# Two output norms of a 1-core transformer kernel, each cut into an early and a late part

## The chip, the core and the metric

One core of a Trainium2 chip runs the whole program as one launch. The metric is device time in microseconds, the median of several runs.

## What is computed

Two transformer blocks over 512 tokens of 1024 features, all float32. Each has an attention whose output is normed and goes through a projection:

```python
# block 1
o = concat([rms_norm(oa, g_out_a), rms_norm(ob, g_out_b)], axis=-1)   # two halves of 512 features
x = x + gate_m * (o @ w_out)                                          # then routing and 32 experts
# block 2
o = diff_attention(q, k_all, v_all, lam)                              # 8 heads of 128 features
o = rmsnorm(o, subln_g) * (1.0 - lam_init)                            # a norm for each head
y_attn = o.reshape(B, L, ATTN_OUT) @ w_branch_attn                    # then gates, w_out, PEER experts
```

`oa` comes from a sparse attention (top 128 keys chosen by an index score), `ob` from a forgetting attention.

## The kernel before

The program is a row of blocks, one for each stage, and each block ends with a barrier of all engines. Within a block every engine has its own instruction list, and semaphores order the lists. The token rows lie in `k.o` as 4 tiles (`TT`) of 128 tokens by 1024 features; the products want them feature by feature, as 8 chunks (`KC`) of 128 features by 512 tokens. A float32 product is done in three, from a high and a low part of either operand (`split_products`, lines 195 to 197).

Attention loops (`attention_stage`, `diff_attention_stage`). Each has n = 32 units of a pair of heads, or one head, by one token tile. The loop runs over t with the steps of one unit staggered: score at t, exponential at t (ScalarE, L927 or L2307), turn of the probabilities at t-2 (L777, L2212), copy of the turned ones (ScalarE, `copy_turned`, L935, L2315), weighing with the values at t-3 (L790, L2221), copy of the result to `k.o` at t-4 (VectorE, L825, L2262), its square and sum at t-5 (ScalarE, `square`, L956, L2327). In the first attention units 0 to 15 are `ob` (features 512 to 1023) and units 16 to 31 are `oa`; in the second the order is head by head, so units 28 to 31 are head 7.

Norm (`HeadNorm`, at the start of `out_projection_stage` and `mix_query_stage`, thus behind the barrier). VectorE sums the squares (L1000, L1002, L1003); ScalarE loads the root's table with an idle activation (L1033) and takes the root (L1035); VectorE inverts it (L1006). Then two engines scale the four token tiles in place: VectorE L1010, ScalarE L1040. TensorE turns all 32 pieces of 128 by 128 into the 8 banks of PSUM (L1025). ScalarE writes each chunk's high part (L1044), VectorE its low part (L1013).

Products. `first_products` does output chunks 0 and 1 together, kc by kc, so that it can follow the parts as they come. It writes banks 0 and 1, so it waits for the parts of chunks 0 and 1 before its first product. Later output chunks go through `chunk_products`. Weights stream through a ring of 4 tiles of 1 MB, each serving two output chunks. ScalarE splits off a tile's high part (`high_part`, L169), Pool its low part (`low_part`, L176), the latter raising `w_ready`, and SyncE loads the next tile (L145). In ScalarE's list the high part of the stage's second tile stands behind `norm.scalar`.

In the first out-projection SyncE also loads at the block's start: the routing weights, small tables, two experts (`w_expert_in` 2 x 2 MB, `w_expert_down` 2 x 1 MB, L1083, L1085), and then, once the rows are read (`norm.rows_read`), the table `before` (L1087) and the ring. VectorE at L1146 and TensorE at the bias product L1124 wait for all six of the small loads, `before` among them. Behind L1124 TensorE has the first routing logits (L1117), then output chunk 2, logits, chunk 3, and so on.

`keep_going` issues products of ones into an unused bank.

## Time and profile before

| quantity | value |
|---|---|
| median of 3 runs | 2797.2 us (2794.76 to 2803.7) |
| the profiled execution, its own time | 2801.7 us |
| its span in the trace | 2799.9 us |
| TensorE busy | 2669.2 us (95%) |
| VectorE busy | 1797.7 us (64%) |
| ScalarE busy | 1075.5 us (38%) |
| GpSimd (Pool) busy | 927.1 us (33%) |
| mean granted TensorE clock | 0.973 of 2.4 GHz |

Read it from the last column of a group of rows inward: a timeline row gives when a group of like instructions began, how long it took, and, in brackets, how long the engine sat idle ahead of it and what released it. TensorE is busy nearly always, so the place to look is where it is not. Matmul ends are modelled: a wide product shows 0.39 us but the next one starts 0.23 us after it. PEclk is the granted clock, 1.00 for 2.4 GHz and 0.50 for 1.2 GHz.

### The profile page before, as it was taken

What the parts mean: (1) busy time and instruction counts of PE and PEld (TensorE: products, weight loads), DVE (VectorE), ACT (ScalarE), POOL (GpSimd) and SP (SyncE); (2) the same over time, 40 slices, a digit from 0 to 9 for tenths busy, and PEclk for the clock granted to TensorE, in tenths of its full rate; (3) what the DMA queues carried; (4) which work ended last, traced back from release to release, by engine and by line L of the source; (5) the groups of instructions that cost most, each with busy time, mean ns of one, the idle gap of its engine ahead of it and who ended that gap; (6) DMA issues with size and microseconds to landing.
All of it is one profiled execution on the core that took longest, in us unless ns stands there. A gap on an engine that the chain in (4) does not pass through costs nothing. (4 is left out here: it accounts for less than half of the span.)

```text
span 2799.9 us, 37231 instructions
## 1 busy us (share of the span) xinstructions
PE 2669.2 (95%) x14205; PEld 2187.1 (78%) x14209; DVE 1797.7 (64%) x3171; ACT 1075.5 (38%) x1724; POOL 927.1 (33%) x468
## 2 busy tenths in 40 slices
PE   8997998889999999999899999999999999999998
PEld 5776775333477878878787899999999988888887
DVE  7958432111142538439744199997998967888987
ACT  3225734222243322147633233344555533333333
POOL 0011122222224330121142257886323233455542
PEclk9996999999999999999999999999999999999999
DMA  8830048999633345300322146886689799999995
GB/s 347 312 118 1 1 155 314 418 404 375 263 118 120 135 159 196 135 16 1 121 90 92 61 153 254 294 296 221 224 309 322 291 365 390 375 400 386 396 406 198
DMA packets 135470, 646.30 MB, mean 231 GB/s; under 512 B 21537, under 2 KB 22433, under 8 KB 91041
## 3 DMA queue, kind: packets, MB, share of 16 engines
q1 hardware_dynamic: 86224, 485.11, 46.0%
q0 software_dynamic: 48384, 158.38, 15.0%
q8 instruction: 85, 1.39, 0.2%
q10 hardware_dynamic: 720, 0.96, 0.1%
q14 instruction: 57, 0.46, 0.1%
HBM read 620.25 MB, written 75.50 MB: 248 GB/s over the span
## 5 line engine op out<-in xcount | busy, mean ns | idle before, releaser
L195 PE MATMUL psum<-h_hi,w_hi 128*128 128x384 f32 (+1 forms) x1808 | 665.9, 368 | 21.8 <-DVE h_lo L575 5.3
L197 PE MATMUL psum<-h_hi,w_lo 128*128 128x384 f32 (+1 forms) x1808 | 653.0, 361 | 0.0
L196 PE MATMUL psum<-h_lo,w_hi 128*128 128x384 f32 (+1 forms) x1808 | 652.2, 361 | 0.0
L176 POOL TENSOR_TENSOR w_lo<-ring,w_hi 128x2048 fp32r<-128x2048 f32 x45 | 211.2, 4693 | 729.7 <-ACT w_hi L169 546.4
L195 PEld LDWEIGHTS psum<-h_hi,w_hi 128*128 128x128 f32 x1808 | 342.8, 190 | 56.6 <-issue 27.0
L197 PEld LDWEIGHTS psum<-h_hi,w_lo 128*128 128x128 f32 x1808 | 342.2, 189 | 34.0
L196 PEld LDWEIGHTS psum<-h_lo,w_hi 128*128 128x128 f32 x1808 | 342.8, 190 | 32.7 <-issue 1.9
L2589 ACT ACTIVATE w_hi<-ring 128x2048 fp32r<-128x2048 f32 x127 | 242.5, 1909 | 214.6 <-PE psum L197 193.5
L195 PE MATMUL psum<-w_hi,a_hi 128*128 128x512 f32 x768 | 301.1, 392 | 3.9 <-DVE w_lo L2597 3.1
L197 PE MATMUL psum<-w_hi,a_lo 128*128 128x512 f32 x768 | 300.1, 391 | 0.0
L196 PE MATMUL psum<-w_lo,a_hi 128*128 128x512 f32 x768 | 300.1, 391 | 0.0
L2597 POOL TENSOR_TENSOR w_lo<-ring,w_hi 128x2048 fp32r<-128x2048 f32 x40 | 191.2, 4781 | 93.2 <-ACT w_hi L2589 91.7
L2628 POOL DMA_INDIRECT rows<-in_peer_u,row_index x88 | 131.1, 1489 | 261.7 <-DVE rows L2643 243.2
L2597 DVE TENSOR_TENSOR w_lo<-ring,w_hi 128x2048 fp32r<-128x2048 f32 x87 | 198.8, 2285 | 17.1 <-ACT w_hi L2589 17.1
L3227 ACT ACTIVATE a_hi<-hid_tiles 128x768 fp32r<-128x768 f32 x64 | 54.2, 847 | 348.4 <-PE psum L197 315.6
L1515 PE MATMUL psum<-w_expert_in,x_turn 128*64 128x512 f32 x768 | 171.5, 599 | 13.1 <-issue 10.9
L169 ACT ACTIVATE w_hi<-ring 128x2048 fp32r<-128x2048 f32 x64 | 122.3, 1912 | 135.7 <-PE psum L197 105.6
L195 PEld LDWEIGHTS psum<-w_hi,a_hi 128*128 128x128 f32 x768 | 145.0, 189 | 34.4 <-issue 4.6
L197 PEld LDWEIGHTS psum<-w_hi,a_lo 128*128 128x128 f32 x768 | 144.9, 189 | 30.2
L196 PEld LDWEIGHTS psum<-w_lo,a_hi 128*128 128x128 f32 x768 | 144.9, 189 | 30.1
L2628 POOL DMA_INDIRECT more_rows<-in_peer_v,row_index x73 | 114.6, 1569 | 119.6 <-DVE row_work L2653 102.3
L1515 PEld LDWEIGHTS psum<-w_expert_in,x_turn 128*64 128x64 f32 x768 | 58.0, 138 | 122.5 <-issue 121.6
(493 smaller groups left out, 4641.1 us busy)
## 6 DMA issues: line engine op xcount, KB each, us to landing
ring<-in_weights SPq DMA_DIRECT2D x199, 1024.0 KB
w_expert_in<-in_experts_in SPq DMA_DIRECT2D x32, 2048.0 KB
hid_dram<-hid_acts SPq DMA_DIRECT2D x64, 384.0 KB
gates_dram<-block_gates SPq DMA_DIRECT2D x24, 1024.0 KB, 14.9
hid_tiles<-hid_dram SPq DMA_DIRECT2D x62, 384.0 KB
gate_tiles<-gates_dram SPq DMA_DIRECT2D x15, 1536.0 KB, 13.0
o<-in_ada_later SPq DMA_DIRECT2D x16, 1024.0 KB, 6.3
w_expert_down<-in_experts_down SPq DMA_DIRECT2D x16, 1024.0 KB
```

What stands on the lines that cost most here:

```text
L169: k.nc.scalar.activation(parts(k, n)[0], slot(k, n), ACT.Copy).then_inc(k.w_high, 1)
L176: eng.tensor_tensor(lo, slot(k, n), hi.bitcast(F32), ALU.subtract).then_inc(k.w_ready, 1)
L195: k.nc.tensor.matmul(out, hi, x_hi, start=start, stop=False)
L196: k.nc.tensor.matmul(out, hi, x_lo, start=False, stop=False)
L197: return k.nc.tensor.matmul(out, lo, x_hi, start=False, stop=stop)
L1515: mm = nc.tensor.matmul(k.psum[j * HALF:(j + 1) * HALF, in_banks[s % 2]], x_turn[:, s % 2, c, j * HALF:(j + 1) * HALF], w_in[s % 2][:, j, ...
L2589: k.nc.scalar.activation(parts(k, n)[0], slot(k, n), ACT.Copy).then_inc(k.w_high, 1)
L2597: eng.tensor_tensor(lo, slot(k, n), hi.bitcast(F32), ALU.subtract).then_inc(k.w_ready, 1)
L2628: pool.indirect_dma_start(row_buffer(k, j), None, k.d["peer_u" if j < PAIRS else "peer_v"], bass.IndirectOffsetOnAxis(ap=k.row_index[:, pi ...
L3227: nc.scalar.activation(a_hi[:, r % 2].rearrange(flat), hid[:, r % 2], ACT.Copy).then_inc(a_high, 1)
```

## The change

The norm is cut in two. In the first attention the early part is the half `ob`, in the second the heads 0 to 6; the late part is the rest. The early part's sum, root, reciprocal, scaling and turns move into the last steps of the attention's loop, ahead of the barrier (`sum_early`, `load_root`, `root_early`, `invert_early`, `scale_early_by_scalar`, `turn_early`). In the first attention the square of unit 27 is put one step later to make room for the table load. Behind the barrier four products of ones are issued, the early chunks' high and low parts are made, and the late part's sum, root, reciprocal and scaling stand among them. `first_products` goes through the chunks in the order early, late; the late turns stand on TensorE ahead of step 2 (first norm, 16 turns) or of step 5 (second norm, 4 turns). Chunks are turned into the bank of their place in that order. The small tiles of the norm use memory of tiles that are idle at that time. No DMA is added or removed; SyncE's lists are as before.

```diff
-def first_products(k, pe, outs, tile, source, done, ready):
+def first_products(k, pe, outs, tile, source, done, norm, turn_late_at):
 
 
     wait_split(k, pe, tile)
     hi, lo = parts(k, tile)
-    for kc in range(KC):
-        ready(min(kc + 1, KC - 1))
+    for step, kc in enumerate(norm.order):
+        if step == turn_late_at:
+            norm.turn_late(pe)
+        norm.split(pe, max(step, 1))
         for c, out in enumerate(outs):
             at = (c * KC + kc) * P
-            mm = split_products(k, out, hi[:, at:at + P], lo[:, at:at + P], source[0][:, kc], source[1][:, kc], kc == 0, kc == KC - 1)
-            if kc == KC - 1:
+            mm = split_products(k, out, hi[:, at:at + P], lo[:, at:at + P], source[0][:, kc], source[1][:, kc], step == 0, step == KC - 1)
+            if step == KC - 1:
                 mm.then_inc(done, 1)
...
+    norm = k.norm = HeadNorm(k, k.squares[:], k.head_total, k.vecs[:, G_OUT:G_OUT + KC], range(1, 2), ((2, 3), (2, 3)))
...
                         turn(t - 2)
                     if t >= DEEP:
                         weigh(t - DEEP)
+                norm.turn_early(pe)
 
             @block.vector
             def _(dve):
...
+                    if t == n:
+                        dve.wait_ge(square_done, 2 * first_sparse)
+                        norm.sum_early(dve)
+                    if t == n + 2:
+                        norm.invert_early(dve)
+                        for i in norm.by_vector(norm.early_by_scalar):
+                            norm.scale_by_vector(i, norm.early)
...
-                    if t > DEEP + 1:
+                    if t == n:
+                        norm.load_root()
+                    if t == n + 1:
+                        norm.root_early(act)
+                        square(t - DEEP - 3)
+                    if t == n + 3:
+                        norm.scale_early_by_scalar(act)
+                    if t > DEEP + 1 and t != n:
                         square(t - DEEP - 2)
     k.again = [Again(square_done, 2 * n), Again(exped, 2 * n)] + [
         Again(sem, n) for sem in (scored, maxed, turned, turned_copied, weighed)] + [Again(out_copied, n - first_sparse)]
...
+    def __init__(self, k, squares, total, gain, early, by_scalar, gain_scale=1.0):
+        self.k, self.squares, self.total, self.gain, self.gain_scale = k, squares, total, gain, gain_scale
+        self.early_by_scalar, self.late_by_scalar = by_scalar
+        self.groups = squares.shape[2]
+        self.width = D // self.groups
+        per_group = KC // self.groups
+        self.early, self.late = early, range(early.stop, self.groups) if early.start == 0 else range(0, early.start)
+        self.order = [g * per_group + c for part in (self.early, self.late) for g in part for c in range(per_group)]
+        self.n_early = len(self.early) * per_group
+        self.gains, self.idle = k.head_gains, k.head_idle
+
+    def part(self, view, groups):
+        return view[:, :, groups.start:groups.stop]
+
+    def rows(self, t, groups):
+        return self.k.o[:, t, groups.start * self.width:groups.stop * self.width].rearrange("p (g n) -> p g n", g=len(groups))
+
+    def sum_squares(self, groups):
+        nc, total = self.k.nc, self.part(self.total, groups)
+        if self.squares.shape[-1] > 1:
+            self.k.vstep(nc.vector.tensor_reduce(total, self.part(self.squares, groups), AX.X, ALU.add))
+        nc.vector.tensor_scalar(total, total, 1.0 / self.width, EPS, ALU.mult, ALU.add).then_inc(self.k.head_norm_sems[0], 1)
+
+    def invert(self, dve, groups, half):
+        std_ready, rooted = self.k.head_norm_sems[0], self.k.head_norm_sems[5]
+        total = self.part(self.total, groups)
+        dve.wait_ge(rooted, 2 * self.turn + half + 1)
+        self.k.nc.vector.reciprocal(total, total).then_inc(std_ready, 1)
+        dve.wait_ge(std_ready, 4 * self.turn + 2 * half + 2)
+
+    def scale_by_vector(self, t, groups):
+        rows = self.rows(t, groups)
+        rstd = self.part(self.total, groups)[:, t].unsqueeze(2).broadcast_to([P, len(groups), self.width])
+        self.k.nc.vector.tensor_tensor(rows, rows, rstd, ALU.mult).then_inc(self.k.head_norm_sems[1][self.turn], 1)
+
+    def scale_by_scalar(self, t, groups):
+        for g in groups:
+            part = self.k.o[:, t, g * self.width:(g + 1) * self.width]
+            ins = self.k.nc.scalar.activation(part, part, ACT.Copy, scale=self.total[:, t, g:g + 1])
+        ins.then_inc(self.k.head_norm_sems[2][self.turn], 1)
+
+    def by_vector(self, by_scalar):
+        return [t for t in range(TT) if t not in by_scalar]
+
+    def sum_early(self, dve):
+        self.sum_squares(self.early)
+        self.k.vstep(self.k.nc.vector.tensor_scalar(self.gains, self.gain, self.gain_scale, None, ALU.mult))
+
+    def invert_early(self, dve):
+        self.invert(dve, self.early, 0)
+
+    def load_root(self):
+        self.k.nc.scalar.activation(self.idle, self.k.eps[:, 0:1], ACT.Sqrt)
+
+    def root(self, act, groups, half):
+        std_ready, rooted = self.k.head_norm_sems[0], self.k.head_norm_sems[5]
+        total = self.part(self.total, groups)
+        act.wait_ge(std_ready, 4 * self.turn + 2 * half + 1)
+        self.k.nc.scalar.activation(total, total, ACT.Sqrt).then_inc(rooted, 1)
+
+    def root_early(self, act):
+        self.root(act, self.early, 0)
+
+    def scale_early_by_scalar(self, act):
+        act.wait_ge(self.k.head_norm_sems[0], 4 * self.turn + 2)
+        for t in self.early_by_scalar:
+            self.scale_by_scalar(t, self.early)
+
+    def turn_rows(self, pe, chunks, by_scalar, scaled_earlier):
+        k, nc = self.k, self.k.nc
+        _std_ready, scaled, scaled_by_scalar, turned, _copied, _rooted = k.head_norm_sems
+        by_vector = self.by_vector(by_scalar)
+        for t in (*by_vector[:-1], *by_scalar, by_vector[-1]):
+            if t in by_vector:
+                pe.wait_ge(scaled[self.turn], scaled_earlier[0] + by_vector.index(t) + 1)
+            else:
+                pe.wait_ge(scaled_by_scalar[self.turn], scaled_earlier[1] + by_scalar.index(t) + 1)
+            for c in chunks:
+                mm = nc.tensor.transpose(k.psum[:, self.order.index(c), t * P:(t + 1) * P], k.o[:, t, c * P:(c + 1) * P], k.ident[:])
+                if t == by_vector[-1]:
+                    mm.then_inc(turned, 1)
+
+    def turn_early(self, pe):
+        self.turn_rows(pe, self.order[:self.n_early], self.early_by_scalar, (0, 0))
+
+    def turn_late(self, pe):
+        self.turn_rows(pe, self.order[self.n_early:], self.late_by_scalar, (TT - len(self.early_by_scalar), len(self.early_by_scalar)))
+
+    def begin(self, split):
+        self.parts, self.high_turn, self.k.activations = split, self.k.activations, self.k.activations + 1
+        k, nc = self.k, self.k.nc
+
+        def low(step):
+            c = self.order[step]
+            dve.wait_ge(k.activation_high, KC * self.high_turn + step + 1)
+            nc.vector.scalar_tensor_tensor(self.parts[1][:, c], k.psum[:, step], self.gains[:, c:c + 1], self.parts[0][:, c].bitcast(F32),
+                                           ALU.mult, ALU.subtract).then_inc(k.head_norm_sems[4], 1)
+
+        self.sum_squares(self.late)
+        low(0)
+        self.invert(dve, self.late, 1)
+        low(1)
+        for t in self.by_vector(self.late_by_scalar):
+            self.scale_by_vector(t, self.late)
+        for step in range(2, KC):
+            low(step)
+        k, nc = self.k, self.k.nc
+
+        def high(step):
+            c = self.order[step]
+            act.wait_ge(k.head_norm_sems[3], KC * self.turn + step + 1)
+            nc.scalar.activation(self.parts[0][:, c], k.psum[:, step], ACT.Copy, scale=self.gains[:, c:c + 1]).then_inc(k.activation_high, 1)
+
+        high(0)
+        self.root(act, self.late, 1)
+        high(1)
+        if self.late_by_scalar:
+            act.wait_ge(k.head_norm_sems[0], 4 * self.turn + 4)
+        for t in self.late_by_scalar:
+            self.scale_by_scalar(t, self.late)
+        for step in range(2, KC):
+            high(step)
+
+    def split(self, pe, step):
+
+        pe.wait_ge(self.k.head_norm_sems[4], KC * self.turn + step + 1)
...
-        norm = HeadNorm(k, sb, "out1_norm", (k.h_hi, k.h_lo), 2, k.vecs[:, G_OUT:G_OUT + KC], k.squares[:], (0, 1), (2, 3), (0, 2, 1, 3))
+        norm = k.norm
+        norm.begin((k.h_hi, k.h_lo))
...
-                norm.tensor(pe)
-                first_products(k, pe, [k.psum[:, c] for c in range(2)], first, (k.h_hi, k.h_lo), done, lambda kc: norm.split(pe, kc))
+                keep_going(k, 7, 4)
+                first_products(k, pe, [k.psum[:, c] for c in range(2)], first, (k.h_hi, k.h_lo), done, norm, 2)
...
+    norm = k.norm = HeadNorm(k, k.squares2[:], k.squares2[:].rearrange("p t g n -> p t (g n)"), k.vecs[:, SUBLN:SUBLN + 1].broadcast_to([P, KC]),
+                             range(0, DIFF_HEADS - 1), ((3,), ()), 1.0 - LAMBDA_INIT)
...
+                pe.wait_ge(out_copied, n - 1)
+                norm.turn_early(pe)
...
+                    if t == n + 1:
+                        dve.wait_ge(square_done, n - TT)
+                        norm.sum_early(dve)
+                    if t == n + 2:
+                        norm.invert_early(dve)
+                        norm.scale_by_vector(0, norm.early)
+                        norm.scale_by_vector(1, norm.early)
+                    if t == n + 3:
+                        norm.scale_by_vector(2, norm.early)
 
             @block.gpsimd
             def _(pool):
...
                         copy_turned(t - 2)
+                    if t == n + 1:
+                        norm.root_early(act)
+                    if t == n + 3:
+                        norm.scale_early_by_scalar(act)
                     if t > DEEP + 1:
                         square(t - DEEP - 2)
+                    if t == n:
+                        norm.load_root()
 
 
 def mix_query_stage(k, mix, tail, choice):
...
-    norm = HeadNorm(k, lambda name, shape: mix.enter_context(nc.sbuf_tensor(name, shape, F32)), "out2_norm", (branch_hi, branch_lo), DIFF_HEADS,
-                    k.vecs[:, SUBLN:SUBLN + 1].broadcast_to([P, KC]), k.squares2[:], (0, 1, 2), (3,), (0, 1, 3, 2), 1.0 - LAMBDA_INIT)
+    norm = k.norm
+    norm.begin((branch_hi, branch_lo))
...
-            norm.tensor(pe)
-            first_products(k, pe, [k.psum[:, c] for c in range(2)], first, (branch_hi, branch_lo), branch_done.sem, lambda kc: norm.split(pe, kc))
+            keep_going(k, 7, 4)
+            first_products(k, pe, [k.psum[:, c] for c in range(2)], first, (branch_hi, branch_lo), branch_done.sem, norm, 5)
...
+        k.head_total, k.head_gains, k.head_idle = k.pick_weight[:].rearrange("p a t -> p t a"), k.route_bias[:, 0:KC], k.route_bias[:, KC:KC + 1]
```

## Rows read from the trace of the kernel before

**Rows 1.** Timeline, TensorE, first norm: start us, us, engine line, xcount, [idle before]

```profile
347.85 3.27 PE L790 MATMUL psum<-small,attn_probs_t 128*128 128x64 f32 x28
355.69 5.88 PE L1025 MATMUL psum<-ident,o 128*128 128x128 f32 x32 [4.57 <-DVE o L1010]
363.12 0.47 PE L195 MATMUL psum<-h_hi,w_hi 128*128 128x512 f32 x1 [1.55 <-DVE h_lo L1013]
...
374.40 1.94 PE L1124 MATMUL psum<-w_route,o 128*128 128x36 f32 x16
...
379.25 0.63 PE L195 MATMUL psum<-h_hi,w_hi 128*128 128x512 f32 x1
```

**Rows 2.** Timeline, TensorE, second norm

```profile
1367.24 2.84 PE L2221 MATMUL psum<-v,diff_probs_t 128*128 128x128 f32 x24
1374.56 5.05 PE L1025 MATMUL psum<-ident,h 128*128 128x128 f32 x32 [4.48 <-DVE h L1010]
1381.16 0.47 PE L195 MATMUL psum<-h_hi,w_hi 128*128 128x512 f32 x1 [1.55 <-DVE h_lo L1013]
...
1391.92 0.39 PE L197 MATMUL psum<-h_hi,w_lo 128*128 128x512 f32 x1
```

**Rows 3.** Timeline, ScalarE, first norm

```profile
346.01 0.80 ACT L935 ACTIVATE attn_probs_t<-psum 128x768 f32<-128x768 f32 x1
...
348.05 1.02 ACT L935 ACTIVATE attn_probs_t<-psum 128x1024 f32<-128x1024 f32 x1 [0.77 <-PE psum L777]
...
351.82 0.24 ACT L956 ACTIVATE h<-o 128x64 f32<-128x64 f32 x1
351.96 0.19 ACT L956 ACTIVATION_READ_ACCUMULATOR h<-o 128x1 f32 x1
352.47 1.28 ACT L1033 ACT_TABLE_LOAD   x1 [0.32 <-PEq L715]
...
354.41 2.56 ACT L1040 ACTIVATE o<-o,out_norm_rstd 128x512 f32<-128x512 f32 x4 [0.35 <-DVE out_norm_rstd L1006]
```

**Rows 4.** Timeline, SyncE's queue, first norm

```profile
352.47 0.33 SPq L1078 DMA_DIRECT2D w_route<-in_w_route  x1
```

**Rows 5.** Windows: stretch, its us, busy us (count) of five engines, PEclk, DMA share, GB/s

```profile
372.00:374.00 2.00, 2.00 (x10) 1.59 (x10) 0.00 (x0) 0.00 (x0) 0.12 (x1) 1.00 1.01 411
```

**Rows 6.** Timeline, VectorE, first norm

```profile
349.41 0.29 DVE L825 TENSOR_TENSOR o<-psum,h 128x128 f32<-128x128 f32 x1 [3.15 <-PE psum L790]
...
354.41 2.36 DVE L1010 TENSOR_TENSOR o<-o,out_norm_rstd 128x1024 f32<-128x1024 f32 x2
361.57 5.36 DVE L1013 SCALAR_TENSOR_TENSOR h_lo<-psum,out_norm_gains,h_hi 128x512 fp32r<-128x512 f32 x8 [4.79 <-ACT h_hi L1044]
...
374.28 0.46 DVE L1146 TENSOR_TENSOR w_route_scaled<-w_route,mod 128x288 f32<-128x288 f32 x1 [6.62 <-DMA o<-in_before]
```

**Rows 7.** Windows, around the first norm (columns as in rows 5)

```profile
353.00:354.00 1.00, 0.00 (x0) 0.00 (x0) 0.02 (x1) 0.99 (x3) 0.00 (x0) 0.68 0.45 134
...
376.00:378.00 2.00, 1.71 (x13) 1.60 (x12) 0.86 (x2) 1.66 (x3) 1.42 (x1) 0.81 0.44 180
...
380.00:384.00 4.00, 4.00 (x17) 3.16 (x17) 0.00 (x0) 0.00 (x0) 1.22 (x1) 0.92 0.40 121
```

**Rows 8.** Line 1025: count, duration ns min/median/max, first and last start

```profile
L1025 PEld LDWEIGHTS psum<-ident,o x32: 139/226/229, 355.7 to 361.2; 128*128 128x128 f32 x32
```

**Rows 9.** Timeline, ScalarE, second norm

```profile
1365.70 0.31 ACT L2327 ACTIVATE diff_squared<-h 128x128 f32<-128x128 f32 x1
...
1383.47 1.96 ACT L169 ACTIVATE w_hi<-ring 128x2048 fp32r<-128x2048 f32 x1
```

**Rows 10.** Timeline, VectorE, second norm

```profile
1368.78 0.29 DVE L2262 COPY h<-psum 128x128 f32<-128x128 f32 x1 [1.88 <-PE psum L2221]
...
1373.28 3.50 DVE L1010 TENSOR_TENSOR h<-h,out_norm_rstd 128x1024 f32<-128x1024 f32 x3
```

**Rows 11.** Timeline, Pool, second norm

```profile
1385.50 4.71 POOL L176 TENSOR_TENSOR w_lo<-ring,w_hi 128x2048 fp32r<-128x2048 f32 x1 [42.45 <-ACT w_hi L169]
```

55 lines of the change are left out of this document (removed).

## The prediction

> **What bounds the kernel now.** I first read which engine the pauses belong to. TensorE is busy for nearly the whole span, so what lengthens its work or its pauses lengthens the kernel. Around the first norm its timeline [rows 1] has three parts: its last attention product ends at 347.85 + 3.27 = 351.12, its 32 turns run from 355.69 to 361.57, and the first two chunks of the out-projection run from 363.12 until the narrow product L1124 begins at 374.40. From 351.12 to 363.12, 12.0 us, TensorE does nothing but turns. The second norm [rows 2] looks the same: 1370.08 to 1381.16, 11.1 us.
>
> The second look is at what opens the block after the attention. ScalarE's last square ends at 351.96 + 0.19 = 352.15, and its table load follows at 352.47 [rows 3]: the barrier between blocks costs 0.32 us after the last engine. SyncE issues its first load at that same moment [rows 4], and the loads are what I read third. Six megabytes of expert weights, one megabyte of ring tile and the small `before` table pass through a path that is full: 411 GB/s at the end [rows 5]. VectorE waits 6.62 us at L1146 until `before` is there, at 374.28 [rows 6]. TensorE waits for the same table ahead of L1124, which it reaches at 374.40. So in the first stage two chains end within about 0.1 us of one another: norm and products on TensorE, and the loads since the block opened, 374.28 - 352.47 = 21.8 us long. Shortening the first gains only as far as the second allows.
>
> **First norm: the end of the attention.** DVE's sum of 32 squares that were long ready is three short operations in its spare time. ScalarE's table load (1.28 us) and the small activation behind it take about 1.4 us [rows 3]. They move behind the copy of 346.01 to 346.81, so the next copy starts at 348.22 instead of 348.05 [rows 3]. TensorE first has 12 of its 28 products at 3.27/28 = 0.117 us to do, until 349.25 [rows 1], when that copy is just through: nothing is lost, with no cover left. The Trainium skill, ScalarE: Activation LUTs, section What ACT_TABLE_LOAD costs, adds a drain of about 1.38 us to the 1.28 us of the load, which speaks against a load among attention work. Rows 3 show the load 0.32 us behind ScalarE's last work, barrier included, so no such drain; by the page each block opening would come up to 1.4 us later, and the sum below would end at 2803.9.
>
> DVE then does the root's reciprocal (a small operation, 0.2) and two scalings of 512 columns at half of 2.36/2, 0.6 us each [rows 6], from the last-but-one copy (349.41 + 0.2) on: 349.85 to 351.05. The last copy, which needs the product ending at 351.12, is not moved. ScalarE is the longer one. Between its copy (ends 349.2) and its scalings stand the root (0.2) and the squares of three units, two each at the 0.24 us of L956 [rows 3]: 350.75. Its two rows of 512 columns at 0.64 [rows 3] are ready at 351.4 and 352.0, and the remaining two units of squares end at 352.95 instead of 352.15. TensorE takes row 0 at 351.1, rows 2 and 3 as they come, and then row 1: 16 turns at 0.12 us (the pace of L790 [rows 1]), done at 353.1. With the barrier the block opens near 353.45 instead of 352.47: **+1.0 us**.
>
> **First norm: behind the opening.** DVE waits for a high part (0.7), does the low part (5.36/8 = 0.67 [rows 6]), the reciprocal (0.2) and a second low part: two chunks are ready 2.4 us after the opening. Then 48 products at (374.40 - 363.12)/48 = 0.235 [rows 1], 11.3 us, and 16 turns, 1.9 us. The late scalings end 3.65 us after the opening, hidden by steps 0 and 1; high and low parts of the late chunks hide beside steps 2 and 3. If that cover were gone, a step would wait up to 0.67 us for its low part. TensorE would be through at 353.45 + 15.6 = 369.0, which is 5.4 us earlier than 374.40. But SyncE's whole list has moved with the opening. `before` stands behind the megabytes, so that its issue comes somewhat earlier or later changes nothing, and it lands at 353.45 + 21.8 = 375.25. TensorE, blocked at L1124 with the logits and all later chunks queued behind it, resumes near 375.35: the gain of 5.4 turns into a wait of 6.3 us, and **+0.95 us** of delay.
>
> Then the clock. The granted clock fell to its 1.2 GHz level 2.3 us into the 4.6 us pause of before (0.68 over 353 to 354), and it fell even behind the narrow products L1124 and L1117 (0.81 over 376 to 378, so at 377.2), to come back at 380.6 (0.92 over 380 to 384) [rows 7]. After 6.3 us of pause it is low. L1124's 16 products then take about 0.22 us each instead of half that, since their weight load is the limit (226 ns in most turns, 139 in the fastest, clocked high [rows 8]): +1.7. L1117's eight, partly low before, add 0.4. The wide products lose about what they lost before (0.63 us each instead of 0.40 overlapped, 0.43 us apart instead of 0.235, for some 3 us [rows 1]), +0.1. That is **+2.2 us**; bounds: 0 if the narrow ones run at 2.4 GHz, and +3.7 if the low level lasts as long again over wide products (380.6 - 377.2 = 3.4 us, 0.45 us lost in each). I take 2.2, as rows 7 show that narrow products do not keep the clock up. First stage: +0.95 + 2.2 = +3.15.
>
> **Second norm.** The load of the root table goes behind the square of 1365.70 [rows 9], so the next copy starts at 1367.5 and ends near 1368.4; TensorE's last unit of products is due only from 1368.66 (half of 2.84 after 1367.24 [rows 2]). Hidden; without that cover it would cost up to 0.4. DVE, after the copy at 1368.78, does the reciprocal (0.35), scales two rows of seven heads (3.50/3 x 7/8 = 1.02 each [rows 10]) until 1371.4, and only then copies the last unit; the third row is scaled at 1372.75. ScalarE's seven pieces (0.31 each, like the square of that width [rows 9]) are done by 1371.7. TensorE follows DVE: 28 turns, the last seven from 1373.2 to 1374.05. The block opens at 1374.4 instead of 1371.17: **+3.2 us**.
>
> Behind it: two parts at +2.4, 48 products at (1391.92 - 1381.16)/47 = 0.229 [rows 2], 11.0, and 4 turns, 0.5: through at 1388.3 instead of 1392.15, a gain of 3.9. But the next weight tile waits. ScalarE's high part of the tile, L169, stands behind the norm's eighth high part, and that one now needs the late turns, which TensorE issues between products 30 and 31: at 1374.4 + 2.4 + 30 x 0.229 + 0.4 = 1384.05. Add 0.35 until ScalarE has it, 0.6 for the part, 1.96 for L169 [rows 9], and 0.07 of handing over and 4.71 for Pool's low part [rows 11]: 1391.75. TensorE starts chunk 2 then instead of at 1392.15: **-0.4 us**, behind a pause of 3.4 us. The three loads at the opening shift by 3.2 us too, but VectorE needs them only for the gates, and TensorE asks for the first gate at chunk 4, 11 us later: nothing. The pause in rows 7 took the clock after 2.3 us; I let it fall here too and count 2.7 us of products at the low pace, **+1.2 us** (bounds 0 and 1.5). Second stage: +0.8.
>
> **Sum.** 3.15 + 0.8 = +3.95 us on the profiled execution's 2801.7 us (span 2799.9 and 1.8 around it), whose excess of 4.5 over the median 2797.2 lies within the spread of the runs (up to 2803.7). Against the median: **2801.1 us**. I assume that routing, experts and the later stages move along one for one, as each waits for the block ahead.
>
> **Rivals.** (a) Neither load nor tile binds, and products follow as the new order lets them: -5.4 - 3.9 gives 2787.9. For it: all parts are ready in time. Against: L1146's wait for the load [rows 6]. Chance 0.03. (b) Only Pool's tile binds: -5.4 - 0.4 gives 2791.4. It would need 7.6 MB within 15.6 us, 490 GB/s, and rows 5 show 411. Chance 0.05. (c) Load and tile bind, but the clock holds or is soon back: +0.95 - 0.4 gives 2797.8. For it: four extra products stand at each block's start; against: both pauses lie behind them. Chance 0.2. (d) The slower side: the low clock stays. Between the first stage's chunks stand narrow logits, eight at a time, and if the clock, once lost in the 6.3 us wait, is not given back by the first wide chunk, each microsecond more costs 0.45. From 10 us of extra low clock on, the change is slower by 0.3%: 3.95 + 4.5 = 8.45, 2805.7 or more. Against: before, the clock came back within 3 us of wide products [rows 7]. Chance 0.08. (e) The edit does not do what it says: the early turns wait for the scalings ahead of the barrier and nothing is given back behind it, without loss of clock: +1.0 + 3.2 gives 2801.4, the same time from another cause. Chance 0.04. The forecast has 0.6.
>
> **How the numbers follow.** A measurement of this kernel can tell about 0.3%, 8.4 us, from no change. The forecast, (c) and (e) lie inside. Range: from (c) less the runs' spread of 2 us, 2795.8, to all upper bounds (0.95 + 3.7 - 0.4 + 1.5 = 5.75) with the same 2 us, 2805.0; outside are (a), (b) and most of (d), 0.15. Faster 0.03, same 0.91, slower 0.06.
>
> **What would show it right or wrong.** In the profile of after: the first instructions of the first block near 1.0 us later; TensorE idle about 6 us ahead of the narrow product while VectorE waits for `before`; the narrow sixteen taking 3.6 us; at the second norm the block opening 3.2 us later, and TensorE idle 3.4 us until Pool's low part. The prediction is wrong if TensorE enters the narrow product near 369, if the second chunk there follows without a pause, or if the experts' stage does not start later by what the first stage lost.

## The result

| | median | ratio to before, 95% interval |
|---|---|---|
| before | 2800.8 us (12 runs) | |
| after | 2808.3 us (12 runs, 2804.7 to 2813.7) | 1.0028 [1.0015, 1.0041] |
| after, timed again beside other kernels | 2813.4 us | 1.0038 [1.0022, 1.0053] |

The change makes the kernel slower by about 0.3%: +7.8 us [4.2, 11.5] the first time, where +3.9 was predicted. The forecast of 2801.1 us missed twice over. Its base was low (the three runs it started from had a median of 2797.2; twelve give 2800.8), and the change costs about twice what the sum said. All later comparisons are ratios taken beside runs of the kernel before on the same chip.

The page of the changed kernel, span, busy time and clock, tells little by itself:

```profile
span 2805.8 us, 37277 instructions
...
PE 2676.7 (95%) x14221; PEld 2190.2 (78%) x14225; DVE 1800.3 (64%) x3181; ACT 1075.1 (38%) x1725; POOL 924.8 (33%) x468
...
PEclk9996999999999999989999999999999999999999
```

TensorE's share is the same 95%, and its busy time is 7.5 us longer, of which the added products of ones (1.13 us twice, below) explain 2.3. That hints at instructions that took longer, but stages which the change does not touch are in this sum too. Only the stages one by one can tell.

**First norm after.** Before the times are compared, the two traces must be laid on one another: the attention's last copy but one starts at 345.12 here and at 349.41 in [rows 6], so after stands 4.29 us earlier. TensorE's timeline, columns as in [rows 1]:

```profile
346.83 2.01 PE L1083 MATMUL psum<-ident,o 128*128 128x128 f32 x16
349.28 1.13 PE L129 MATMUL psum<-ones 128*128 128x128 f32 x8 [0.44 <-PEq L718]
351.74 0.47 PE L195 MATMUL psum<-h_hi,w_hi 128*128 128x512 f32 x1 [1.33 <-DVE h_lo L1102]
...
370.60 3.60 PE L1211 MATMUL psum<-w_route,o 128*128 128x36 f32 x16 [4.13 <-DMA o<-in_before]
374.49 1.92 PE L1204 MATMUL psum<-w_route_scaled,x 128*128 128x36 f32 x8 [0.29 <-DVE route_bias L1242]
376.21 0.77 PE L195 MATMUL psum<-h_hi,w_hi 128*128 128x512 f32 x1
```

The chain is the predicted one. The block opens at 349.24, or 353.53 on the clock of before against 352.47 in [rows 4]: +1.06, predicted +1.0. TensorE then reaches the narrow product early and waits 4.13 us for the small table `before`. VectorE's line says the same, and says when the table is there, 370.49 - 349.24 = 21.25 us behind the opening (21.8 in the prediction):

```profile
370.49 2.86 DVE L1233 TENSOR_TENSOR w_route_scaled<-w_route,mod 128x288 f32<-128x288 f32 x1 [8.52 <-DMA o<-in_before]
```

The sixteen narrow products then take 3.60 us instead of the 1.94 of [rows 1]. The windows (columns as in [rows 5]) show the clock that belongs to it, and one spell that the prediction did not have:

```profile
350.00:352.00 2.00, 0.67 (x5) 0.51 (x4) 1.97 (x4) 1.77 (x4) 0.00 (x0) 1.00 0.44 107
352.00:354.00 2.00, 2.00 (x7) 1.52 (x7) 2.00 (x4) 1.33 (x3) 0.00 (x0) 0.58 0.97 184
354.00:356.00 2.00, 2.00 (x7) 1.57 (x6) 0.20 (x1) 0.00 (x0) 0.00 (x0) 0.56 0.90 377
...
370.00:372.00 2.00, 1.40 (x7) 1.43 (x7) 1.51 (x1) 0.00 (x0) 2.00 (x1) 0.50 1.04 430
```

At 352.3 the clock falls to 1.2 GHz during wide products, right behind the short pause at the opening, and is back at 355.7. That slows the first chunks, and so the wait that follows was 4.1 us long and not 6.3. It costs nothing of its own, since the table was late anyway: a second profile of the same kernel, `after_again`, has no such spell (granted clock 1.00 from 352 to 360), waits 5.59 us instead of 4.13, and its stage is as long.

```profile
373.15 3.60 PE L1211 MATMUL psum<-w_route,o 128*128 128x36 f32 x16 [5.59 <-DMA o<-in_before]
```

From the attention's last copy (347.10 here, 351.24 in before) to the third update of x (383.65 and 384.99) the stage takes 36.55 us instead of 33.75: **+2.8 us**, where the prediction had +3.15.

**Second norm after** (4.14 us later than before: the last copy but one is at 1372.92 against 1368.78 in [rows 10]). TensorE, ScalarE and Pool, one fence each:

```profile
1374.71 3.42 PE L1083 MATMUL psum<-ident,h 128*128 128x128 f32 x28 [0.57 <-DVE h L1038]
1378.58 1.13 PE L129 MATMUL psum<-ones 128*128 128x128 f32 x8 [0.44 <-PEq L2276]
...
1395.79 0.50 PE L195 MATMUL psum<-h_hi,w_hi 128*128 128x512 f32 x1 [3.09 <-POOL w_lo L176]
```

```profile
1389.19 1.91 ACT L169 ACTIVATE w_hi<-ring 128x2048 fp32r<-128x2048 f32 x1
```

```profile
1391.18 4.56 POOL L176 TENSOR_TENSOR w_lo<-ring,w_hi 128x2048 fp32r<-128x2048 f32 x1 [44.06 <-ACT w_hi L169]
```

Laid on before, the block opens at 1374.40 (predicted 1374.4), ScalarE begins the tile's high part at 1385.05 (1385.0 by the prediction's terms: 1384.05 + 0.35 + 0.6), Pool's low part ends at 1391.60 (predicted 1391.75), and TensorE's pause is 3.09 us (predicted 3.4). In this execution the mechanism and its places are right. What is not right lies in the microseconds that clock and later stages add. To find them I cut the traces at the same nineteen instructions and compared the lengths of the stages. Differences to the profile of before, in us:

| stage | after | after again | first only | second only |
|---|---|---|---|---|
| last copy of attention 1 to third x update | +2.80 | +2.81 | +3.00 | +0.01 |
| last exponential of attention 2 to last gate | +1.00 | +2.06 | +0.19 | +2.03 |
| to the last copy of the out-projection | +0.02 | +0.67 | +0.01 | +0.67 |
| to the first query copy | +1.57 | +1.63 | -0.07 | +1.62 |

The second and the third row have to be read together. Their border is an instruction of VectorE, whose place against TensorE shifts. Counted on TensorE, at the last product of each output chunk, the delay is +1.02 in after, +2.72 in after again and +2.69 in second only. It is complete at the fifth chunk and stays the same to the end of the out-projection, so the out-projection itself loses nothing. After and after again are one and the same kernel: the second norm's stage costs it 1.0 us in one execution and 2.7 us in another.

Two stages are not in the table. The experts' stage was some 3 to 7 us longer in every later profile than in that of before, in profiles of the uncut kernel too (+6.2 in `before_covered`, which only adds a few cheap products), and the start of the second attention varied by up to 3 us. They vary from one profiled execution to the next without any change in them, so nothing of them is put down to the change here.

### The profile page after: what moved, and what is told of

The parts are those of the page before. It is cut to its first block and busy times, and to the rows that moved or that the text cites. A ratio compares the mean times of both kernels' runs of the same rounds, so it can differ in the third digit from the quotient of the medians.

```text
span 2805.8 us, 37277 instructions
## 1 busy us (share of the span) xinstructions
PE 2676.7 (95%) x14221; PEld 2190.2 (78%) x14225; DVE 1800.3 (64%) x3181; ACT 1075.1 (38%) x1725; POOL 924.8 (33%) x468
## 5 line engine op out<-in xcount | busy, mean ns | idle before, releaser
L176 POOL TENSOR_TENSOR w_lo<-ring,w_hi 128x2048 fp32r<-128x2048 f32 x45 | 210.9, 4688 | 735.1 <-ACT w_hi L169 552.6
```

Source lines behind the costliest of these rows:

```text
L176: eng.tensor_tensor(lo, slot(k, n), hi.bitcast(F32), ALU.subtract).then_inc(k.w_ready, 1)
```

## The experiments

The theory on record was that the first norm costs 3.15 and the second 0.8, from waits that take the place of the ones removed and from the clock that they lose. The rivals were that one norm alone costs it all, that something steady elsewhere does, and, after the first results, that the mere shift of the later stages does.

**One norm alone.** `first_only` leaves the second norm as before, `second_only` the first:

```
# first_only
-    norm.begin(...); keep_going(k, 7, 4); first_products(..., norm, 5)        # second attention
+    norm = OldHeadNorm(...); norm.tensor(pe); old_first_products(...)
# second_only: the same in the first attention
```

> Only the first norm is cut in two, the second is as before. Theory A: +2.8 us against before, nothing measurable in later stages. Theory B: if the experts' stage reacts to the shifted start, +6 us. Whoever reads the edit by its aim would expect about -5 us. In the profile: TensorE through its first products about 4 to 6 us ahead of the narrow product L1211-like and idle until the table `before` is there.

Measured: 1.0013 [0.9997, 1.0028], +3.6 us; its stage +3.00. The first norm's term stands.

> Only the second norm is cut in two, the first is as before. Theory A: +1.0 us against before (block opened 3.2 us later, second output chunk pair started 0.4 us earlier, clock +1.2). Theory B: if the second attention's start is what costs, +3 to +4 us. By its aim about -4 us.

Measured: 1.0017 [1.0002, 1.0031], +4.8 us, where the prediction had 0.8. The two halves add up to the whole (8.4 against 7.8). The second norm is the mis-sized one. In its stage there is the same wait for Pool, and there are two low spells where I had counted one. First `second_only`, then the first of the two places in after, where the clock holds:

```profile
1380.00:1384.00 4.00, 3.61 (x9) 2.84 (x10) 4.00 (x10) 2.15 (x4) 0.00 (x0) 0.60 0.96 406
...
1398.00:1402.00 4.00, 4.00 (x12) 3.08 (x12) 2.66 (x4) 1.96 (x2) 0.00 (x0) 0.59 0.62 244
```

```profile
1380.00:1384.00 4.00, 2.95 (x13) 2.47 (x14) 3.96 (x11) 2.81 (x5) 0.00 (x0) 1.00 0.83 348
```

```profile
1396.80 0.50 PE L195 MATMUL psum<-h_hi,w_hi 128*128 128x512 f32 x1 [3.20 <-POOL w_lo L176]
```

The second is behind the pause, as forecast. The first, at 1380.8, comes as in the first norm right behind the opening. It slows the products ahead of the late turns, and what hangs on them: Pool's low part ends 24.48 us behind the last copy but one (1396.74 - 1372.26), against 22.82 in after (1395.74 - 1372.92), which is the 1.7 us between the two kinds of execution. Of six profiles with this norm cut and its waits left in, four (`second_only`, `after_again`, `early_table`, `second_covered`) have both spells and +2.6 to +2.7 us on TensorE, and two (`after`, `filler`) have the forecast one and +1.0 to +1.1.

**The whole again, and the table early.** `after_again` is the changed kernel, timed beside the others. `early_table` gives the small table a tile of its own and loads it with the other small tables, before the block's megabytes:

```
-        sums, before = spare[:, 2 * D:2 * D + SEQ], spare[:, 3 * D:3 * D + P]
+        sums, before = spare[:, 2 * D:2 * D + SEQ], sb("before_rows", [P, P])[:]
...
-                norm.rows_read(sp)
-                sp.dma_start(before, k.d["before"]).then_inc(consts, 16)
```

> The changed kernel itself once more, for a second profile and a second comparison. Theory A (the cost lies in the two norm stages alone, about 2.8 us in the first and 1.0 us in the second, as the two profiles show, and what the 12 runs show beyond 3.8 us is spread): against the kernel before +2 to +8 us, and in its profile both stages again show +2.8 and +1.0. Theory B (there is a further steady cost of some 4 us elsewhere, in the experts' stage or at the second attention's start, where the one pair of profiles shows +3.1 and +2.5): +7 to +8 us, and the same two places show their loss again.

> The changed kernel with one thing more: the table `before` has a tile of its own and is loaded ahead of the experts' weights, so that neither VectorE nor TensorE waits for seven megabytes. The work is otherwise that of the changed kernel. Theory A: the wait of 4.1 us ahead of the narrow product goes, and with it the low clock of the sixteen narrow products (1.7 us): 5 to 6.5 us less than the changed kernel, so -1 to -3 us against before. If the wait were for something else (the weight tile, VectorE's copy of the shift rows), nothing would change: +7 us against before.

Measured: `after_again` 1.0038 [1.0022, 1.0053], which is +10.6 us and above the range given for it; the stages of its profile account for 7.2 (2.81 + 2.06 + 0.67 + 1.63), and for the rest, which the interval allows to be nothing or more, no row is at hand. `early_table` 0.9992 [0.9978, 1.0006]. Its first stage goes from +2.8 to -7.1 us. On TensorE the narrow product now follows without a pause, and its sixteen and eight take 1.87 and 1.08 us instead of 3.60 and 1.92:

```profile
352.42 0.47 PE L195 MATMUL psum<-h_hi,w_hi 128*128 128x512 f32 x1 [1.33 <-DVE h_lo L1102]
...
365.45 1.87 PE L1209 MATMUL psum<-w_route,o 128*128 128x36 f32 x16
367.61 1.08 PE L1202 MATMUL psum<-w_route_scaled,x 128*128 128x36 f32 x8 [0.29 <-DVE route_bias L1240]
```

From the attention's last copy to the narrow product it is now 17.67 us (365.45 - 347.78) instead of 23.16 (374.40 - 351.24). So it is shown that 5.5 us of norm time, 5.4 in the prediction, are given back behind the opening, and that the load hid them. The stage gains some 1.6 us more, as before itself loses that much in its low spell behind the narrow products [rows 7], which is gone here.

**The table early, without the change.** `before_early_table` makes the same edit to the kernel before.

> The kernel before with only the early table: a control for early_table. In the kernel before TensorE reaches the narrow product 0.1 us behind the table's landing, so moving the load gains nothing on the path: 0 us (within 1.5). If it gains as much as early_table (2 us), then that gain is the table's and not the norm's.

Measured: 0.9997 [0.9980, 1.0014], its stage -0.1. TensorE enters the narrow product when its own chain ends, as the two chains that ended together in [rows 1] and [rows 6] said it must. The gain needs both edits.

**The first norm alone, with the table early.** `first_early_table` is the two edits above in one kernel.

> Only the first norm cut in two, with the early table. Theory A: the first norm's cut alone, with its wait gone, gives what it was meant to: the profile of early_table shows 7.1 us less at the third output chunk than the kernel before, so -5 to -7 us against before. If the second norm's cut in early_table costs nothing, it equals early_table (-2 us).

Measured: 0.9963 [0.9945, 0.9980], median 2792.8 us: the lowest median of all kernels here, and below both kernels of this case.

**Filling the wait.** `filler` lets TensorE work on ones while it waits for the table:

```
+                keep_going(k, 7, 16)
                 pe.wait_ge(scaled, 1)
```

> The changed kernel with 16 products of ones (about 3.8 us) in the wait of 4.1 us ahead of the narrow product of the first projection. It changes nothing but TensorE's activity in the wait. Theory A: the clock holds, the sixteen narrow products take 1.94 instead of 3.60 us and the eight behind them 1.4 instead of 1.9, so the whole is 2 us less than the changed kernel, with up to 3 us less if chunk 2 keeps its clock too. If the clock is no cost: no change.

Measured: 1.0012 [0.9999, 1.0026], stage +1.89 instead of +2.8. TensorE, and the window behind the narrow products:

```profile
367.86 3.73 PE L129 MATMUL psum<-ones 128*128 128x128 f32 x32
...
373.66 1.95 PE L1212 MATMUL psum<-w_route,o 128*128 128x36 f32 x16 [2.06 <-DMA o<-in_before]
```

```profile
376.00:380.00 4.00, 4.00 (x14) 3.52 (x15) 0.49 (x1) 1.01 (x2) 0.00 (x0) 0.50 0.81 332
```

The narrow sixteen take 1.95 us again, so the prediction's term of 1.7 us for them at the low clock holds. The table came when it came. Of those 1.65 us only 0.9 stayed gained in the stage, because the clock fell later instead, over the wide products behind (0.50 in the window 376 to 380), and was low until 382.8, where in after it was back at 379.6.

**Filling the second norm's pauses.** `second_covered` is `second_only` with 43 and 28 ones products where the query stage has 32 and 20; `before_covered` is before with the same:

```
-            keep_going(k, 2, 32)
+            keep_going(k, 2, 43)
...
-            keep_going(k, 2, 20)
+            keep_going(k, 2, 28)
```

> The kernel with only the second norm cut in two, and two pauses of TensorE filled that lie 100 us later, between the out-projection and the query products (43 instead of 32 products of ones, and 28 instead of 20; each fills about 0.23 us of a pause of 2.6 or 2.1 us). In the profiles of all four kernels with the second norm cut, the clock falls in these two pauses and the query products start 1.6 us late; in the two without it, it does not. Theory C (the cut shifts the moments of the pauses against the moments at which the clock can change, and so costs 1.6 us there): 1.6 us less than second_only, no low clock between 1470 and 1515 in the profile, the query's first copy no longer late. Theory D (that loss has another cause, a weight tile or a load that comes later): no change against second_only, the wait for it seen in the profile.

> The kernel before with the same two pauses filled. Theory C: within 0.5 us of the kernel before, since its profile shows no low clock there. If the kernel before loses its clock there in other executions than the profiled one, a gain of up to 1.6 us.

Measured: 1.0019 [1.0008, 1.0029] and 1.0000 [0.9987, 1.0013]. The 1.6 us ahead of the first query copy were gone (-0.07), and 1.63 us came back a stage later, ahead of the first peer set. A filled pause moved the loss and did not lower it. This speaks for the clock as its cause, and against filling as its cure. `before_covered` loses the 1.6 us at neither place.

**Is it the shift?** The query products and what stands just ahead of them are untouched by the change, and yet they came 1.6 us late. `shifted_4`, `_8` and `_12` are the kernel before with 4, 8 and 12 ones products ahead of the last chunk of the out-projection, no other edit:

```
+                if c == KC - 1:
+                    keep_going(k, 2, 4)        # 8, 12
                 hi, lo = parts(k, first_out + c // 2)
```

> The kernel before, nothing cut, with 4 products of ones (0.93 us) ahead of the last chunk of the second output projection: all that follows comes 0.9 us later. Theory F (what costs at the query products is only where the pauses of TensorE fall against the moments at which the granted clock can change, and these hardly move with the program): this shift keeps the pauses clear of it, as in the profile of filler; +0.9 us, query products on time. Theory G (the cut itself makes the loss): +0.9 us as well.

> As shifted_4 with 8 products of ones (1.9 us). Theory F: between the two cases, +1.9 us, or up to +3.5 if the pauses are hit. Theory G: +1.9 us.

> As shifted_4 with 12 products of ones (2.8 us). Theory F: the pauses now fall as in the profiles of the cut kernels; two spells of low clock between the last output chunk and the query products, whose first copy comes 2.8 + 1.6 = 4.4 us late. Theory G: no such spells, +2.8 us.

| kernel | shift put in | extra to first query copy | ratio |
|---|---|---|---|
| shifted_4 | 0.95 | +0.10 | 1.0001 [0.9988, 1.0013] |
| shifted_8 | 1.86 | +1.64 | 1.0015 [1.0001, 1.0028] |
| shifted_12 | 2.74 | +1.62 | 1.0023 [1.0011, 1.0035] |

In the profile a shift of 1.9 us costs 3.5, with nothing of the change in the kernel. The ratios agree, but do not prove it by themselves: the shifts alone would make 1.0003, 1.0007 and 1.0010, and only the last lies outside its interval, and barely. The windows of the query stage, each pair laid where that stage stands in its trace (the second begins 0.6 to 0.9 us behind the first wide product), of before, after, `shifted_4` and `shifted_12` in that order:

```profile
1480.00:1484.00 4.00, 2.67 (x5) 0.89 (x6) 4.00 (x7) 1.89 (x3) 0.00 (x0) 1.00 0.00 0
1498.00:1502.00 4.00, 4.00 (x19) 3.31 (x18) 4.00 (x7) 2.20 (x4) 0.00 (x0) 1.00 0.97 408
```

```profile
1485.00:1489.00 4.00, 2.90 (x4) 1.17 (x5) 4.00 (x7) 1.89 (x3) 0.00 (x0) 0.57 0.00 0
1503.00:1507.00 4.00, 4.00 (x13) 3.15 (x12) 4.00 (x7) 2.19 (x4) 0.00 (x0) 0.62 0.99 420
```

```profile
1481.00:1485.00 4.00, 3.00 (x5) 1.10 (x6) 4.00 (x8) 1.89 (x3) 0.00 (x0) 0.77 0.00 0
...
1499.00:1503.00 4.00, 4.00 (x19) 3.27 (x19) 4.00 (x7) 2.21 (x4) 0.00 (x0) 1.00 0.94 395
```

```profile
1485.00:1489.00 4.00, 2.71 (x3) 1.12 (x4) 4.00 (x7) 1.80 (x3) 0.00 (x0) 0.60 0.00 0
1503.00:1507.00 4.00, 4.00 (x12) 3.12 (x11) 4.00 (x7) 2.19 (x4) 0.00 (x0) 0.59 1.01 426
```

Read the second window of each pair, the one with the wide products. Its PE count is 19 at a clock of 1.00, 13 and 12 at about 0.6. After and `shifted_12` fall there, before and `shifted_4` do not. The low spell of the first window, which `shifted_4` has in part (0.77), costs it no more than the +0.10 of the table. The pause ahead of the products is the same in all, here in before and in after:

```profile
1497.21 0.47 PE L195 MATMUL psum<-h_hi,w_hi 128*128 128x512 f32 x1 [2.12 <-DVE h_lo L2521]
```

```profile
1502.26 0.47 PE L195 MATMUL psum<-h_hi,w_hi 128*128 128x512 f32 x1 [2.12 <-DVE h_lo L2627]
```

A pause of 2.12 us thus loses the clock or does not. A shift is not needed for it. In `before_early_table`, whose query stage is that of before and has nothing put in ahead of it, the first query copy is 1.65 us late too, behind the same pause:

```profile
1507.98 0.47 PE L195 MATMUL psum<-h_hi,w_hi 128*128 128x512 f32 x1 [2.12 <-DVE h_lo L2519]
```

```profile
1508.80:1512.80 4.00, 4.00 (x12) 3.14 (x12) 4.00 (x7) 2.20 (x4) 0.00 (x0) 0.62 0.98 412
```

`filler`, `second_fixed` and `all_waits`, on the other hand, have the second norm cut and lose nothing there (+0.03 to +0.05). So the loss is neither the cut's own nor the shift's own: it falls on an execution or does not, and a cut or a shift changes where the pause lies. How often before itself loses it, one profile for each kernel cannot say.

**The second norm's tile.** The prediction's wait there could be taken away. `tile_sooner` puts ScalarE's high part of the next tile ahead of the norm's last one:

```
-            norm.scalar(act)
+            norm.scalar(act, lambda: next_high(k, act, first, 0, used))
```

> The changed kernel with one step moved: in the second projection ScalarE takes the high part of the second weight tile ahead of the norm's last high part instead of behind it. Theory A: Pool's low part is ready before TensorE is through its first products, the pause of 3.1 us goes, and with it the low clock behind it (1.2 us): 3 to 5 us less than the changed kernel. Rival: VectorE's gates wait for the load of x at that place (6.7 us in the profile of after), and the gain is given back at chunk 4, where TensorE wants the first gate: less than 1 us.

Measured, in 8 runs instead of 12: 1.0031 [1.0017, 1.0044], stage +1.83: nothing gained. Pool's low part ended 6.4 us sooner, measured from the attention's last copy but one (1390.58 - 1374.12 against 1395.74 - 1372.92 in after), and the wait stood one tile further on. TensorE, the waits of VectorE (us, count, mean):

```profile
1409.40 0.47 PE L195 MATMUL psum<-h_hi,w_hi 128*128 128x512 f32 x1 [3.02 <-POOL w_lo L176]
```

```profile
DVE gates_again L2597 <- DMA x<-x_dram: 5.0, 1, 5.0
```

The gates wait 5.0 us for the load of x, which they do not read: gates, u and x count up one semaphore, and the gates wait for all three. ScalarE's part of the third tile is queued behind them. In after that wait is there as well, 6.72 us until 1396.80, and hidden: Pool's tile holds TensorE until 1395.79, and the chunks that need the gates or the third tile are two further on. `tile_and_x` is `tile_sooner` and lets x count on a semaphore of its own, so that the gates wait for two loads:

```
-            for to, source in ((k.gates[:], k.gate_dram), (k.u[:], k.u_dram), (x[:], k.x_dram)):
+            for to, source in ((k.gates[:], k.gate_dram), (k.u[:], k.u_dram)):
                 sp.dma_start(to, source).then_inc(k.moved, 16)
+            sp.dma_start(x[:], k.x_dram).then_inc(loaded, 16)
```

> The changed kernel with the second weight tile's high part taken sooner, as in tile_sooner, and the load of x counted on a semaphore of its own, so that VectorE's gates wait for 4 MB and no longer for 6 MB; only the later update of x waits for x. In tile_sooner TensorE lost the 3.1 us again one tile later (3.0 us for Pool's low part of the third tile, whose high part stands in ScalarE's list behind the gates of chunks 0 and 1). Theory E (that chain, load of x, gates, third tile, gave the gain back): the 3.0 us wait goes, and the kernel is 2 to 4 us faster than tile_sooner. Rival (low clock, not waiting, sets this stage): within 1 us of tile_sooner.

Measured: 1.0004 [0.9990, 1.0018], stage -3.68. The second norm's time was given back, 3.9 us by the prediction's working, once both waits were off.

**All waits off.** `all_waits` joins early table, tile and x; `second_fixed` is `second_only` with tile and x alone.

> The changed kernel with all three waits taken away: the table `before` in its own tile and loaded first, the second tile's high part sooner, and x on its own semaphore. Theory A and E together: early_table was 2 us below the kernel before; 3 to 4 us less for the second stage: 4 to 8 us below before (0.9972 to 0.9985), the first kernel here that is clearly faster.

> Only the second norm cut in two, with its two waits taken away (the second tile's high part sooner, x on its own semaphore). In the profiles of tile_and_x and all_waits the second stage then gives 3.7 us back. Against before: -3.7 us if nothing later takes it, -2 us if the query products are hit by a low clock. The first norm is as before. If it is not faster than before at all, the second cut brings nothing even with its waits gone.

Measured: 0.9968 [0.9955, 0.9981] and 0.9991 [0.9978, 1.0005]. In `all_waits` Pool's first tile and the first gate:

```profile
1379.52 4.68 POOL L176 TENSOR_TENSOR w_lo<-ring,w_hi 128x2048 fp32r<-128x2048 f32 x1 [37.55 <-ACT w_hi L169]
```

```profile
1386.95 0.69 DVE L2596 TENSOR_TENSOR gates_again<-gates_again,psum 128x512 f32<-128x512 f32 x1 [2.05 <-PE psum L197]
```

VectorE now waits for the product and no more for a load. Both stages hold their gains (-7.1 and -3.8), and 1.63 us are lost again to the clock ahead of the peer sets. Against `first_early_table` (0.9963) the second norm adds nothing that can be told: -3.8 + 1.6 = -2.1 us by the stages, and the intervals overlap. `second_fixed`, 0.9991 as a whole, says the same. It loses nothing at the query or peer products, but its stage is at -2.1 and not at -3.7: it has a low spell behind the opening (0.50 from 1379.8 to 1383.2), which `tile_and_x` and `all_waits` have not.

## Why the prediction was wrong, and where it was right

**What bounds the kernel** was right: in both norms the engine rows gave the chain, and the opening, the table, Pool's tile and the pause came within 0.6 us of where they were put in the profile of after.

**First norm, +3.15**: right, +2.8 and +3.0 in three profiles. Its parts, the opening (+1.06), the table's landing (21.25 us for 21.8), the narrow sixteen (3.60 - 1.94 = 1.66 for 1.7), are each in a row. Two terms were off against one another: TensorE entered the narrow product +0.5 us late and not +0.95 (370.60 - 345.12 against 374.40 - 349.41), as the table landed sooner than forecast, and the clock took 2.3 us behind it and not 2.2. The wait was 4.1 us and not 6.3, since a low spell at 352.3 slowed the chunks ahead of it; the end of the chain, a load, did not move by that.

**Second norm, +0.8**: this is the failed step, at about +4.3 in `second_only` by the stages and +4.8 [0.6, 8.7] by the whole. It failed in two terms. The first is the clock term of +1.2, bounds 0 and 1.5, which knew of one low spell, behind the pause. There it was right, and the stage came to +1.02 in after. But in four of six profiles a second spell stood behind the opening, ahead of the tile, and the stage came to 2.6 or 2.7 on TensorE: 1.6 to 1.7 us that no term and no bound had. The second is the sentence that later stages move along one for one. At the query products 1.56 to 1.65 us are lost in after and in eight other profiles, of which `shifted_8`, `shifted_12` and `before_early_table` have nothing of the cut in them. Both losses fall on some executions and not on others, so that this size is what single profiles show, and no fixed price of the change. By the stages after loses 5.4 us in all (2.8 + 1.0 + 1.6) and `after_again` 7.2, where the medians say 7.8 [4.2, 11.5] and 10.6 [6.2, 14.8].

**Three loads at the opening: nothing.** Right in after, by half a reason. I argued with the time until TensorE asks for the first gate, and that did cover VectorE's wait of 6.72 us for x. What I left out is that ScalarE's high part of the third tile stands behind the gates. It cost nothing only because Pool's tile held TensorE until 1395.79; with that tile moved it cost the 3.0 us of `tile_sooner`.

**The rivals.** Neither load nor tile binding, 2787.9, was refuted by after, and `all_waits` shows what it would have been worth: 0.9968, 9.0 us less than before where the working had 9.3 (by the stages -7.1 - 3.8 + 1.6 = -9.3, so it agrees by errors that cancel: the first stage gave more than 5.4, and the clock took 1.6). The slower side, (d), had the right cause and the wrong place: not a low clock that stays within the first stage, but further short spells, in the second norm's stage and at the query products. The case that nothing is given back, (e), falls with `early_table` and `tile_and_x`. The drain of 1.38 us behind a table load that the Trainium skill, ScalarE: Activation LUTs, section What ACT_TABLE_LOAD costs, states is not in this trace. ScalarE, after, with the load now between two copies of turned probabilities:

```profile
342.53 1.28 ACT L1057 ACT_TABLE_LOAD   x1
343.83 0.20 ACT L1057 ACTIVATE route_bias<-eps 128x1 f32<-128x1 f32 x1
343.94 1.01 ACT L946 ACTIVATE attn_probs_t<-psum 128x1024 f32<-128x1024 f32 x1
```

The copy ahead of it ends at 342.51, and the one behind it begins at 343.94: 1.43 us for the load and its small idle activation together. So the 1.4 us of the prediction's working stand.

**The base.** Of the distance from 2801.1 to 2808.3, 3.6 us are the median of before, which three runs put at 2797.2 and twelve at 2800.8. The width of those three, 9 us, and not 2 us should have gone into the range, since the spread of the base counts whole where a time and not a ratio is forecast.

**Still open**: what `after_again` loses beyond its stages; how often the kernel before loses its clock at the query products; what the second norm is worth once its waits are off; and why the experts' stage differs by some 3 to 7 us between the profile of before and all others.

## What to carry to other kernels

When work is moved ahead of a block and given back behind it, look for whatever starts at the block's opening and does not get shorter: here a 64 KB table queued behind megabytes, and a tile whose preparation stands behind the late part. Free that first (`first_early_table`, 0.9963), for the same edit without it costs time. Where a semaphore counts several loads, give the one that is needed last its own: a wait for data that nobody reads may be hidden today and bind tomorrow. And do not count later stages as moving one for one where TensorE pauses for some 2 us in them: price a lost clock at about 1.6 us each time, put it into the range, and take more than one profile before you call it a cost of the change.

## What the runs showed of the hardware that I had not expected

**The same pause costs clock or does not.** In its profiles the kernel before, moved by 0.95 us, loses nothing at the query products; moved by 1.86 or 2.74 us it loses 1.6 more, and in `before_early_table` it does so without such a shift, each time behind a pause of 2.12 us that is unchanged. The granted clock of the products there falls from 1.00 to about 0.6. The place from the program's start does not settle it: behind the pause that ends at 1505.17 in `first_only` the clock is 1.00 (1506 to 1510), behind the one that ends at 1505.02 in `tile_sooner` it is 0.61 (1505.8 to 1509.8). By a rule of the Trainium skill (TensorE: Matmul & The Clock Gate, section What's actually happening), the timing of the clock gate is its own and is not set by the program's start; this pair agrees.

**VectorE held by Pool.** An operation of VectorE that takes 0.46 us in [rows 6] took 2.86 us in after, and in `early_table` a cast of 128 columns took 4.69 us, for 0.22 in before. Beside each stands a low part of Pool that ends at about the same time:

```profile
361.34 4.69 DVE L1233 CAST before_half<-before_rows 128x128 bf16<-128x128 f32 x1
```

```profile
361.23 4.72 POOL L176 TENSOR_TENSOR w_lo<-ring,w_hi 128x2048 fp32r<-128x2048 f32 x1 [37.22 <-ACT w_hi L169]
```

In after it is 370.49 + 2.86 = 373.35, with Pool's L176 running from 368.49 to 373.03. The Trainium skill, SBUF — State Buffer, section Who interferes with whom, says that the two engines share a port pair. A cast can hold it for its whole instruction while the other engine waits, or wait in its turn, and an operation of VectorE with two SBUF inputs contends with a Pool operation that reads SBUF. The two pairs agree with it. That it is the cause was not tried by itself. The trace counts such time as busy, so a long mean of a small operation is a wait to look for.
